# Laying out 96 tokens four times over for the expert rows: transposes and 12 copies, or matmuls with 32 columns

## The reference

```
x = x + g1 * y
h2 = rmsnorm(x, norm2_g[l]) * (1.0 + sc2) + sh2
...
q = (hb @ w_q).reshape(TOKEN_BLOCK, PEER_HEADS, 2, PEER_DKEY // 2)
s = jnp.einsum('thpd,hpkd->thpk', q, sub_keys)       # 8 heads, 2 halves, 128 keys
top_s, top_i = lax.top_k(s, PEER_TOPK)               # 16 of 128
cand_s = top_s[:, :, 0, :, None] + top_s[:, :, 1, None, :]
best_s, best_pos = lax.top_k(cand_s, PEER_TOPK)      # 16 of 256
expert = take_along_axis(cand_i, best_pos)
act = gelu(einsum('thkd,td->thk', u_tab[expert], hb))
out = einsum('thk,thkd->td', softmax(best_s) * act, v_tab[expert])
```

## Time and profile before

| | us |
|---|---|
| median of 3 runs (lowest to highest) | 919.97 (918.93 to 922.51) |
| the profiled execution | 919.97 |
| its span, first to last instruction | 918.1 |
| PE busy | 874.5 |
| DVE busy | 533.3 |
| ACT busy | 281.3 |
| POOL busy | 264.1 |

### The profile page before, as it was taken

One profiled execution on the slowest core, in us unless ns is written; L12 is line 12 of the kernel. 1 busy time (PEld: TensorE's weight loads), 2 busy tenths in 40 slices (PEclk: granted clock), 3 DMA queues, 4 the chain that ended last, 5 costly groups with the idle time before them and its releaser, 6 DMA issues.

```text
span 918.1 us, 17679 instructions
## 1 busy us (share of the span) xinstructions
PE 874.5 (95%) x6640; PEld 824.6 (90%) x6640; DVE 533.3 (58%) x1035; ACT 281.3 (31%) x683; POOL 264.1 (29%) x242
## 2 busy tenths in 40 slices
PE   5789999999999999999998999999999999999995
PEld 3568997578798999999998999999999999999995
DVE  2445414767289949995455888888333444334437
ACT  3453223864634111112114888881000000000002
POOL 0020000320324043356353333365332233232220
PEclk9589999999999999999999999999999999999999
DMA  9766584115257789999999999999999999999993
GB/s 369 306 229 230 184 321 154 76 49 228 92 183 255 231 270 412 410 409 410 410 409 409 409 394 334 322 332 363 409 409 409 409 409 409 409 409 408 408 409 126
DMA packets 74558, 294.28 MB, mean 321 GB/s; under 512 B 9218, under 2 KB 9346, under 8 KB 67972
## 3 DMA queue, kind: packets, MB, share of 16 engines
q1 hardware_dynamic: 37444, 161.24, 46.0%
q0 software_dynamic: 28416, 100.78, 28.9%
q10 hardware_dynamic: 8640, 31.46, 8.6%
HBM read 290.73 MB, written 1.05 MB: 318 GB/s over the span
## 4 chain that ended last, share of the span: by engine, by line
PE 77%; DMA 9%; DVE 5%; ACT 5%; issue 2%; POOL 1%; DVEq 0%; SPq 0%; ACTq 0%
PE bank L920 30%; PE bank L864 25%; PE bank L873 4%; PE bank L593 4%; DMA A<-in_peer_u,row_expert 4%; PE bank L595 4%; PE bank L594 4%; DMA A<-in_w_in 2%; DMA stage<-in_peer_u_t 2%; DVE ring_low L1309 1%; PE bank L613 1%; DVE gate_buf L1277 1%; POOL A L1665 1%; PE bank L603 1%; PE bank L807 1%
## 5 line engine op out<-in xcount | busy, mean ns | idle before, releaser
L864 PE MATMUL bank<-A,stage 128*128 128x160 f32 x2048 | 289.4, 300 | 3.7 <-issue 1.5
L864 PEld LDWEIGHTS bank<-A,stage 128*128 128x128 f32 x2048 | 280.0, 190 | 7.4 <-issue 6.9
L920 PE MATMUL bank<-A,stage 128*128 128x160 f32 x2048 | 278.3, 299 | 0.0
L920 PEld LDWEIGHTS bank<-A,stage 128*128 128x128 f32 x2048 | 278.2, 190 | 0.0
L1391 DVE SCALAR_TENSOR_TENSOR sum<-A,row_gate,sum 128x1024 f32<-128x1024 f32 x81 | 104.1, 1285 | 132.3 <-DMA A<-in_peer_v,row_expert 130.9
L1681 POOL DMA_INDIRECT A<-in_peer_u,row_expert x80 | 91.8, 1147 | 134.9 <-DVE row_dot L1378 126.7
L1681 POOL DMA_INDIRECT A<-in_peer_v,row_expert x84 | 82.4, 981 | 166.3 <-DVE sum L1391 148.9
L1378 DVE CUSTOM_DVE_ANT_0 A<-A 128x1024 f32<-128x1024 f32 x80 | 97.4, 1221 | 44.6 <-DMA A<-in_peer_u,row_expert 44.4
L1211 ACT ACTIVATE A<-bank 128x480 f32<-128x480 f32 x1 | 0.6, 572 | 276.3 <-PE bank L920 276.3
L1143 ACT ACTIVATE A<-bank 128x160 f32 (+1 forms) x88 | 26.6, 304 | 157.3 <-PE bank L864 139.2
L595 PE MATMUL bank<-h_hi,ring_low 128*128 128x256 f32 x256 | 72.8, 284 | 0.0
(11 more groups left out here) (237 smaller groups left out, 1205.3 us busy)
## 6 DMA issues: line engine op xcount, KB each, us to landing
stage<-in_peer_u_t SPq DMA_DIRECT2D x128, 512.0 KB
stage<-in_peer_v SPq DMA_DIRECT2D x68, 512.0 KB
stage<-in_peer_v ACTq DMA_DIRECT2D x60, 512.0 KB
A<-in_ada_w SPq DMA_DIRECT2D x24, 1024.0 KB, 6.9
A<-in_w_in SPq DMA_DIRECT2D x11, 1024.0 KB, 4.8
A<-in_w_q SPq DMA_DIRECT2D x8, 1024.0 KB, 5.6
A<-in_w_out SPq DMA_DIRECT2D x4, 1024.0 KB, 6.5
stage<-in_bias_mask SPq DMA_DIRECT2D x1, 2048.0 KB, 12.5
```

What stands on the lines that cost most here:

```text
L864: mm = pe.matmul(o, stage[j][:, k * P:(k + 1) * P], H2[:, k, 0:ND], start=(k == 0), stop=(k == KD - 1))
L920: mm = pe.matmul(bank[b][:, n * ND:(n + 1) * ND], stage[c % SLOTS][:, m * P:(m + 1) * P], A3[:, c, :], start=(c == 0 and n == 0), stop=(c ...
```

## The change

The two row steps become six, `("rows_turned", 0)` to `("rows_turned", 5)`: two for each group of 32 tokens, one per half of the width. A step is 16 matmuls: for each of four blocks `k` of `H2`, four matmuls with the same 32 tokens as stationary columns and the identity as moving operand, one for each column position of the array, so that the result stands four times over the partitions of the bank. ACT copies the bank straight into `h2_rows`, six copies of 128 by 512. Four steps stand where the two stood, behind `keys` 2. The last two, for the group whose place is taken until the last query block, stand between `keys` 6 and `keys` 7. `turned_tokens`, the 12 transfers and all waits for `rows_laid` are gone.

```
--- before.py
+++ after.py
@@ schedule
         if b == 3:
-            steps += [("rows_turned", n) for n in range(2)]
+            steps += [("rows_turned", n) for n in range(4)]
         if b in (4, 5):
             ada(4 * G2 + b - 2)
     turn()
+    steps += [("rows_turned", n) for n in range(4, 2 * SUBS)]
     steps.append(("keys", PH - 1))
@@ SP, behind the loads of u chunks 0 to 7
-                    sp.wait_ge(rows_copied, 2)
-                    for s in range(SUBS):
-                        if s == SUBS - 1:
-                            old, use = place[("w_q", PH - 1)]
-                            sp.wait_ge(bank_full[old], use + 1)
-                        for q in range(4):
-                            sp.dma_start(h2_rows[q * SUB:(q + 1) * SUB, s, :],
-                                         turned_tokens[ND1 + s * SUB:ND1 + (s + 1) * SUB, :]).then_inc(rows_laid, 16)
@@ PE, turned_rows
                 o = opened(pe, ("rows_turned", n))
+                s = n // 2
+                tokens = slice(ND + s * SUB, ND + (s + 1) * SUB)
                 for m in range(4):
-                    mm = pe.transpose(o[:, m * P:(m + 1) * P], H2[:, 4 * n + m, T - P:T], ident)
+                    k = 4 * (n % 2) + m
+                    for q in range(4):
+                        mm = pe.matmul(o[q * SUB:(q + 1) * SUB, m * P:(m + 1) * P], H2[:, k, tokens], ident,
+                                       start=True, stop=True, tile_position=(0, q * SUB))
                 mm.then_inc(fill_sem(("rows_turned", n)), 1)
@@ ACT
                     o = full(act, (kind, n))
-                    act.activation(turned_tokens[:, n * 512:(n + 1) * 512], o[:, :], ACT.Copy).then_inc(rows_copied, 1)
-                    act.wait_ge(rows_copied, n + 1)
-                    act.sem_inc(free_sem((kind, n)), 1)
+                    act.activation(h2_rows[:, n // 2, n % 2 * 512:n % 2 * 512 + 512], o[:, :], ACT.Copy)\
+                       .then_inc(free_sem((kind, n)), 1)
@@ ACT ahead of chunk 8, DVE ahead of the first dot, POOL ahead of the first gather
-            act.wait_ge(rows_laid, 16 * 4 * SUBS)
-                if n == 0:
-                    dve.wait_ge(rows_laid, 16 * 4 * SUBS)
-            pool.wait_ge(rows_laid, 16 * 4 * SUBS)
```

More of the change, by code:

```diff
@@ L368, in build @@
         h2_rows = A[:, 0:SUBS * D].rearrange("p (s d) -> p s d", s=SUBS)
-        turned_tokens = A[:, 15360:16384]
         with ExitStack() as views:
@@ L471, in build @@
         row_full = [sem(f"row_full{s}") for s in range(WIDE_GATHER)]
-        rows_copied, rows_laid = sem("rows_copied"), sem("rows_laid")
         folded, act_out, dve_out = sem("folded"), sem("act_out"), sem("dve_out")
```

## The result

The changed kernel takes 925.64 us in the median of 8 runs (924.38 to 928.08), the kernel before 920.32 us (918.93 to 922.51). The ratio is 1.0064, with a 95% interval of 1.0047 to 1.0083, so +5.9 us by the ratio (the two medians are 5.3 us apart). The forecast was +3.1 us, 923.1 us, in a range of 918.9 to 930.5. The direction and most of PE's share came out as forecast; 2.8 us were missing by the ratio, 2.2 by the medians, and the narrower range that the prediction calls its own, 921.5 to 925, was missed by 0.6 us. The profiled execution took 926.95 us with a span of 925.2, against 919.97 and 918.1, +7.0.

The account below looks back on a forecast made before the run. PE bounds the kernel, with slack beside full DMA from 390 to 498 us. PE's delay of 2.75 + 1.88 + 0.2 = 4.83 us, less the 1.74 us wait, gives 919.97 + 3.1 = 923.1 us, range 918.9 to 930.5.

Parts of the forecast that it names:

- What goes: On SP's queue up to 297 us: taking away the 12 copies gains 0, for the waiters and for the bytes.
- The narrow matmuls: Row steps on PE: full overlap, 0.87 us a step; +2.75 us behind query block 3, +1.88 behind keys 6.
- Rival (a): Row steps on PE: a narrow record costs its slot whatever its columns, +11.1 us on PE, 929.4 us; chance 0.20.
- How the shift travels to 296 us: From query block 4 to chunk 0: nothing is absorbed, so PE arrives 4.83 us later.
- the 0.2 us for the copy of step 5: Ahead of chunk 0: PE waits for ACT's copy of the last row step, 0.2 us, between 0 and 0.6.
- The expert list: On the top-k path: the list comes 2.75 us later, taking only the delay of the first four row steps.
- Rival (c): Ahead of block 4 or chunk 0: a new copy wait holds PE or DVE one or two us, 925.5 us; chance 0.08.
- At 497 us: At the first gate: PE at 500.76 comes after the one-hot at 500.42, its wait is gone, +3.1 us instead of 4.8.
- the upper end of its own range: Up to the first gate: DVE's path moving by as much as PE would bring the time to 925 us.
- The term that I entered as -1.74: At the first gate: PE's 1.74 us wait for DVE's first one-hot vanishes and is credited against PE's delay.
- Behind 497 us: From the first gate to 904 us: PE is full, so the 3.1 us reach the end.
- Rival (b): Up to 497 us: bytes set the stretch, so 1.57 MB less ends it earlier, -1.1 us, 918.9 us; chance 0.15.

Follow-up runs that it names:

- the first four experiments: Kernel before without transfers 921.21 us, kernel before with PE's narrow matmuls added 928.49; changed kernel with six steps behind keys 7 927.19, with inner loops exchanged 935.41.

## Why the prediction was right in its range and short in its sum

- **What goes: 0.** Shown, by taking the transfers away alone (ratio 1.000).
- **The narrow matmuls.** Full overlap of the four positions was the right choice: 3.63 and 1.89 us against 3.62 and 1.88. Rival (a), a slot per record whatever its columns, is out: a record cost 3.63 / 128 = 0.028 us. The exchanged loops show what it rests on, the order of the list. The fixed cost of about 62 ns per matmul that I cited from the Trainium skill, "TensorE: Matmul & The Clock Gate", section "Wait — 56ns, not 53.3ns?", isn't seen here even per matmul of the code: 3.63 / 64 = 57 ns with going in and out. It is stated there for decoding in software, and no run shows which decoding this program had. The other floor cited there, about 25 ns from start to start, isn't seen from one record to the next: the first four start at 261.873, 261.880, 261.886 and 261.893, 7 ns apart. On average, 28 ns a record, it isn't broken.
- **How the shift travels to 296 us.** Forecast 4.83, measured 5.03 (5.15 against keys 0). The 0.2 us for the copy of step 5 were not paid (keys 7 pass to chunk 0 in 0.99 us, keys 6 to the narrow steps in 0.98); in their place PE's delay grew from 2.81 us at block 4 to 3.08 at keys 6. The expert list: forecast 2.75, measured 3.1. Rival (c), a new wait for a copy, is not in the trace.
- **At 497 us: the step that failed.** "The one-hot 497.67 + 2.75 = 500.42. PE is now last and its wait is gone: +3.1 us in place of 4.8." The one-hot came 5.3 us later, and the wait grew to 3.6. Two things were wrong in it. The top-k path doesn't run free of PE from the expert list on: it waits for an exponential behind chunk 55 and for transposes behind chunk 71, so it takes over PE's shift. That DVE's path might move by as much as PE is named in the prediction as the upper end of its own range, without this reason and without the clock. And behind these waits stands the real bound, the transfers: in eight kernels with all loads and rows the first gate came 200.7 to 202.1 us behind chunk 0, whatever was moved between them, and 191.9 and 192.0 with half the bytes of u. PE's 5.4 us of slack there were a symptom of full transfers, not a reserve. The term that I entered as -1.74 was +0.3.
- **Behind 497 us.** "Behind that PE is full to 904, so the 3.1 us reach the end" held for what arrives at the gate, but I had no term for the clock. In this execution it fell behind the longer wait, 1.7 us. It did so also with the work of before on PE: in the kernel with the transfers taken away PE waited 2.85 us at the gate, and gate 0 to gate 2 took 9.2 us. So this is no steady price of the change. The profiled execution of before, with a wait of 1.74, was spared; it also had a stall of PE near 440 us that none of the other kernels with the transposes at chunk 72 shows (from chunk 64 to chunk 72 it took 20.3 us against 18.0 in all of them). That this let the gathers catch up is likely and not shown. How often its other executions see the fall is open. There is a hint: of the 17 executions of the kernel before beside the first four experiments, the eight with a mean granted clock of 0.977 or 0.978 have a median of 921.8 us, the nine with 0.980 or 0.981 one of 920.3. But the clock is also low at times in the first 240 us, and these figures don't tell where it fell.
- **The sum.** Forecast: 4.83 - 1.74 = 3.1. Measured 5.9 by the ratio, 5.3 by the medians: 5.2 of PE, and 0.1 to 0.7 for the clock and for what runs scatter, which I can't part. The halved loads, where neither wait nor fall disturbs the first gate, put the whole price at 5.4. That the time lay inside the stated range owes something to the width of the range: the credit at the gate, more than a third of PE's shift, was not there.
- **Rival (b)** named the right resource with the wrong arrow. The transfers do set the stretch up to 497, but the copies lay outside it.

No version found here beats the kernel before. The nearest, with the exponential and the transposes earlier, is the same within 0.2%.

## What to carry to other kernels

A transfer that nobody waits for can't be improved by doing its work on the engine that bounds the kernel, however cheap the matmuls: here 5 us of well-overlapped TensorE work bought nothing. Before slack further on is entered as a credit, look at what the other path waits for on its way; a path that meets the bound engine at two points, or shares its transfers with it, brings the shift along. And if the DMA is at 1.0 in a stretch with idle PE, ask whether its length is a matter of bytes, as it was here, where a wait taken away only moved; halving the bytes is the test.

## What the runs showed of the hardware that I had not expected

- The records of f32 matmuls with 32 columns each, on the four column positions and next to each other in the list, start in fours within 0.02 us, and the next four follow 0.11 us later. A matmul leaves two records, so four matmuls cost 0.23 us together (64 matmuls, 128 records, in 3.63 us). With four matmuls of one position in a row, the same 64 took 8 us.
- PE's clock fell to its lower level around waits of 2.9, 3.6, 3.6, 5.2 and 5.7 us at the first gate, and not with the one of 1.74, nor where there was none. The price, read from gate 0 to gate 2 against 6.2 us, was 1.7 us (both waits of 3.6), 2.9 (wait of 2.9), 2.5 (wait of 5.2) and 3.0 (wait of 5.7): it doesn't grow with the wait. It is half of that part of the low stretch that lies behind the start of the gate. In the kernel with the transfers taken away the clock was at 0.50 from 495.87 to 502.70, and the gate started at 496.70: (502.70 - 496.70) / 2 = 3.0. In the changed kernel it was at 0.50 from 504.04 to 507.45, all of it behind the gate's start at 502.99: (507.45 - 504.04) / 2 = 1.7.
